# Values of the second attention for all heads at once, token-major and through HBM, with new orders at the opening, between passes and at the end

## The reference, cut to what matters

```python
h = rmsnorm(x, norm_g); proj = h @ w_in            # w_in: 2048 x 10304
aq, ak, av, ag, cq, ckv, kr, bg, mg = split(proj)
# branch A: differential attention, 8 heads, keys/queries 2 x 64, values 128 wide
# branch B: latent attention, 8 heads
q  = (rmsnorm(cq,  q_norm_g)  @ w_uq ).reshape(heads, 128 + 64)    # 512 -> 8 x 192
kv = (rmsnorm(ckv, kv_norm_g) @ w_ukv).reshape(heads, 128 + 128)   # 512 -> 8 x (keys, values)
ob = softmax((q_nope k_nope + rope(q_rope) rope(kr)) * scale) @ values
yb = (ob * silu(bg)) @ w_ob
merged = sigmoid(ga) * ya + sigmoid(gb) * yb
out = rmsnorm(x + merged @ w_out, final_g)
```

## Time and profile before

| | |
|---|---|
| median of 3 runs | 1468.38 us (1468.36 to 1468.58) |
| profiled execution, its own time | 1470.03 us |
| its span, first to last instruction | 1468.2 us |
| mean granted TensorE clock | 0.999 |
| TensorE busy | 98% |
| VectorE, ScalarE, GpSimd busy | 72%, 41%, 3% |
| moved by DMA | 203.75 MB |

### The profile page before, as it was taken

The page is one execution under the profiler, slowest core; times in us unless marked ns, Lnnn a source line. Parts: engine busy times, 40 slices in busy tenths (PEclk is TensorE's granted clock), DMA queues, the critical chain, the costliest instruction groups (busy, mean ns, idle before and its releaser), DMA issues.

```text
span 1468.2 us, 18187 instructions
## 1 busy us (share of the span) xinstructions
PE 1444.1 (98%) x6812; PEld 1201.6 (82%) x6812; DVE 1053.5 (72%) x1423; ACT 606.1 (41%) x786; POOL 45.0 (3%) x58
## 2 busy tenths in 40 slices
PE   7999999999999999999999999999999999999997
PEld 6887888888888888888888888888888888887876
DVE  6867888888877777777776557777777353488956
ACT  5534354444345344453443344443454122324434
POOL 0000000000000011101110000000000000000000
PEclk9999999999999999999999999999999999999999
DMA  8448575767563222322222332222232435517574
GB/s 288 144 150 281 170 259 179 252 194 227 173 189 100 80 79 74 91 79 79 79 72 81 92 87 79 65 72 58 68 121 69 158 116 157 201 44 239 177 245 185
DMA packets 179024, 203.75 MB, mean 139 GB/s; under 512 B 18960, under 2 KB 134800, under 8 KB 178192
## 3 DMA queue, kind: packets, MB, share of 16 engines
q1 hardware_dynamic: 173168, 189.25, 41.8%
q10 hardware_dynamic: 5792, 13.63, 2.4%
HBM read 185.02 MB, written 17.83 MB: 138 GB/s over the span
## 4 chain that ended last, share of the span: by engine, by line
PE 89%; DVE 5%; DMA 3%; SPq 1%; issue 1%; ACT 1%; POOL 0%; DVEq 0%; POOLq 0%; ACTq 0%
PE duo L1959 27%; PE duo L1961 27%; PE duo L1960 27%; PE duo L2012 2%; DMA start_y<-start_columns 1%; PE duo L1986 1%; PE duo L1989 1%; DVE o_lo L1348 1%; DMA spare<-in_w_in_dram 1%; PE duo L2045 1%; SPq L600 1%; PE duo L2039 1%; DMA m_raw<-in_w_in_dram 1%; PE duo L2008 0%; PE duo L2007 0%
## 5 line engine op out<-in xcount | busy, mean ns | idle before, releaser
L1959 PE MATMUL duo<-h_hi,w_hi 128*128 128x512 f32 x656 | 261.0, 398 | 0.3 <-DVE k_hl L1230 0.3
L1961 PE MATMUL duo<-h_hi,w_lo 128*128 128x512 f32 x656 | 256.1, 390 | 0.0
L1960 PE MATMUL duo<-h_lo,w_hi 128*128 128x512 f32 x656 | 255.8, 390 | 0.0
L1225 DVE TENSOR_TENSOR w_lo<-w_raw,w_hi 128x1024 fp32r<-128x1024 f32 (+1 forms) x130 | 156.1, 1202 | 134.6 <-ACT w_hi L707 134.4
L707 ACT ACTIVATE w_hi<-w_raw 128x1024 fp32r<-128x1024 f32 (+1 forms) x130 | 135.5, 1043 | 203.7 <-DMA w_raw<-in_w_ob_dram 65.9
L790 ACT ACTIVATE m_hi<-m_raw 128x2048 fp32r<-128x2048 f32 (+1 forms) x58 | 101.8, 1758 | 143.1 <-PE duo L1961 55.6
L1961 PEld LDWEIGHTS duo<-h_hi,w_lo 128*128 128x128 f32 x656 | 123.1, 188 | 26.9
L1959 PEld LDWEIGHTS duo<-h_hi,w_hi 128*128 128x128 f32 x656 | 123.3, 188 | 24.2 <-DVE k_hl L1230 0.7
L1960 PEld LDWEIGHTS duo<-h_lo,w_hi 128*128 128x128 f32 x656 | 123.5, 188 | 23.5
L1348 DVE TENSOR_TENSOR m_lo<-m_raw,m_hi 128x2048 fp32r<-128x2048 f32 (+2 forms) x59 | 121.0, 2051 | 16.9 <-ACT m_hi L790 16.8
L1959 PE MATMUL duo<-m_hi,h_hi 128*128 128x512 f32 x320 | 126.1, 394 | 4.7 <-ACT post_z L878 2.2
(11 more groups left out here) (293 smaller groups left out, 2846.8 us busy)
## 6 DMA issues: line engine op xcount, KB each, us to landing
m_raw<-in_w_in_dram SPq DMA_DIRECT2D x94, 512.0 KB, 4.6
w_raw<-in_w_in_dram SPq DMA_DIRECT2D x164, 256.0 KB, 3.2
o_raw<-in_w_out_dram SPq DMA_DIRECT2D x34, 512.0 KB, 4.9
w_raw<-in_w_oa_dram SPq DMA_DIRECT2D x32, 256.0 KB, 3.4
sig<-gates SPq DMA_DIRECT2D x8, 1024.0 KB, 6.3
w_raw<-in_w_ob_dram SPq DMA_DIRECT2D x32, 256.0 KB, 3.3
spare<-in_w_in_dram SPq DMA_DIRECT2D x13, 512.0 KB, 4.5
h_raw<-in_w_in_dram SPq DMA_DIRECT2D x13, 512.0 KB, 5.2
```

The costliest lines, as they stand in the source:

```text
L1225: dve.tensor_tensor(w_lo[:, piece.slot, 0:cols], w_raw[:, piece.slot, 0:cols], w_hi[:, piece.slot, 0:cols].bitcast(F32), ALU.subtract).the ...
L1959: pe.matmul(dst, lhs_hi, rhs_hi, start=start, stop=False)
L1960: pe.matmul(dst, lhs_hi, rhs_lo, start=False, stop=False)
L1961: return pe.matmul(dst, lhs_lo, rhs_hi, start=False, stop=stop)
```

## The change

Values of attention B are no longer made per head. Four steps are added to the C steps (20 to 24): with the compressed keys and values as the stationary operand and four heads' value columns of w_ukv (512 wide) as the moving one, they give values token-major for heads 0 to 3 and 4 to 7 in banks of their own. ScalarE copies the banks and stores them in the HBM tensor that held the first attention's values; SP loads each head's strip from there to `vb_raw`, and ScalarE and VectorE split it. The compressed keys and values come ahead of the queries in the C steps. The matmuls of the values in `b_up`, the copy to vT and its transposes go. Beside that orders change: at the opening (x in six parts, weight blocks 0 and 3 split by halves, blocks 1 and 2 loaded ahead of x's tiles 2 and 3), at the ends of the gate groups (`keep_p2` before `merge_hi`), at the starts of passes (`LOW_FIRST`), in the last steps of the output projection, and at the end (the middle store by ScalarE's queue, a shorter variance).

```diff
-A_STEPS, C_STEPS, B_STEPS = 6, 20, 4
+A_STEPS, C_STEPS, B_STEPS = 6, 24, 4
+VB_STEP = 20
+VB_BANKS = ((6, 7, 2, 3), (4, 5, 6, 7))
+B_READS = 3
+        slots = range(M_RAW if shared else OWN_RAW)
+        if st.n == len(steps) - L_STEPS - 1:
+            slots = range(OWN_RAW, M_RAW)
+LOW_FIRST = (V_STEPS, V_STEPS + 1, OUT0 + L_STEPS, OUT0 + L_STEPS + 1, MID_SPLIT)
-TURN_X_AT = {0: (6, 7), 2: (8, 9, 10, 11), 3: (12, 13, 14, 15)}
+TURN_X_AT = {0: (6,), 1: (7,), 2: (8, 9, 10, 11), 3: (12, 13, 14, 15)}
+HALVED = (0, 3)
-X_PARTS = [(0, slice(0, D_MODEL)), (1, slice(0, D_MODEL // 2)), (1, slice(D_MODEL // 2, D_MODEL)),
-           (2, slice(0, D_MODEL)), (3, slice(0, D_MODEL))]
+X_PARTS = [(0, slice(0, D_MODEL // 2)), (0, slice(D_MODEL // 2, D_MODEL)), (1, slice(0, D_MODEL // 2)),
+           (1, slice(D_MODEL // 2, D_MODEL)), (2, slice(0, D_MODEL)), (3, slice(0, D_MODEL))]
...
 SP
+            def b_values_in(h):
...
+                sp.wait_ge(v_lo_ready, h + HEADS)
+                sp.dma_start(vb_raw[:, :, :], v_d[:, bass.ds(h * P, P)].rearrange("(t p) c -> p t c", p=P)
+                             ).then_inc(v_in, 16)
             def b_head(h, odd):
                 for s in range(2):
                     block_piece(Piece(B0 - 2 + s, h, B_STEPS), w_in, 8 * s, h * P + BG)
+                b_values_in(h - 1)
                 up_pieces(h, odd)
             for i, (t, cols) in enumerate(X_PARTS):
-                if i == 3:
+                if i == X_SPLIT + 2:
                     merge_piece(0)
...
-                if i == 4:
                     merge_piece(1)
+                    merge_piece(2)
...
 ScalarE
+            def keep_vb(g):
...
+                for i in range(TOK):
+                    t = (i + 2 * g) % TOK
...
+                    act.activation(vb_keep[:, t, :], bank[VB_BANKS[g][t]][:, :], ACT.Copy).then_inc(v_kept, 1)
+                    act.wait_ge(v_kept, TOK + TOK * g + i + 1)
+                    act.dma_start(v_d[t * P:(t + 1) * P, g * SEQ:(g + 1) * SEQ], vb_keep[:, t, :]).then_inc(v_out[t % 2], 16)
             for s in range(C_STEPS):
+                split_hi(Piece(C0 + s + AHEAD), HALF_PIECE if s == C_STEPS - 1 else 2 * HALF_PIECE)
...
+                if s in (VB_STEP + 1, VB_STEP + 3):
+                    keep_vb((s - VB_STEP) // 2)
             def merge_step(n):
+                if n + 1 in SECOND_END:
+                    keep_p2(MERGE[n].g)
                 if n + AHEAD < N_MERGE:
                     merge_hi(n + AHEAD)
-                if n + 1 in SECOND_END:
-                    keep_p2(MERGE[n].g)
...
 VectorE
             def merge_step(n):
+                if n + 1 < N_MERGE and n in LOW_FIRST:
+                    merge_lo(n + 1)
                 if n + AHEAD < N_MERGE and not ends:
                     merge_sums(n + AHEAD)
-                if n + 1 < N_MERGE:
+                if n + 1 < N_MERGE and n not in LOW_FIRST:
                     merge_lo(n + 1)
...
                 if s == 2 and cur:
-                    dve.wait_ge(used, h * B_STEPS + (B0 + 2))
-                    if prev:
-                        dve.wait_ge(v_turned, h)
-                    dve.tensor_copy(vT[:, :], ACC[0][:, :]).then_inc(acc_read, 1)
...
-                if n >= MID_END - 2:
-                    merge_lo(n + 2)
+                if n == MID_END - 2:
+                    merge_lo(MID_END)
...
             out_u3_c22()
+            merge_lo(MID_END + 1)
             merge_lo(MID_END + 2)
...
 TensorE
+            def token_values(g, half):
+                piece = Piece(C0 + VB_STEP + 2 * g + half)
+                pe.wait_ge(lo_ready, piece.after(0))
+                if not half:
+                    pe.wait_ge(c_lo_ready, LT)
+                for i in range(TOK):
+                    t = (i + 2 * g) % TOK
...
+                    for k in range(2):
+                        hi, lo = tile(piece, k * SEQ, SEQ)
+                        kt = 2 * half + k
+                        last = three(bank[VB_BANKS[g][t]][:, :], c_hi[:, kt, q], c_lo[:, kt, q], hi, lo,
+                                     kt == 0, kt == LT - 1)
...
                 if s == 2 and cur:
                     scores_b(h, 0, prev)
                     scores_b(h, 1, prev)
-                    pe.wait_ge(acc_read, h * 4 + (A_READ0 + 13))
...
-                    turn(vT, TR, v_turned)
...
-                up(piece, 0, ACC[1], 1).then_inc(k_up, 1)
-                pe.wait_ge(acc_read, g + 1)
-                up(piece, P, ACC[0], 1).then_inc(used, 1)
+                up(piece, 0, ACC[1], 0, P).then_inc(used, 1)
                 b_extras(1, h, pair, True, prev)
             def b_gate(h, pair, prev):
                 for s in range(2):
                     if s == 0:
-                        pe.wait_ge(acc_read, h * 4 + (A_READ0 + 12))
+                        pe.wait_ge(acc_read, h * B_READS + (A_READ0 + 12))
```

More of the change, by code:

```diff
@@ L109, in merge_steps @@
         shared = HALF_K + V_SPLIT <= st.n < n_merge - M_RAW or n_merge + L_STEPS <= st.n < len(steps) - L_STEPS
-        st.raw = min(range(M_RAW if shared else OWN_RAW), key=lambda slot: free[slot])
+        slots = range(M_RAW if shared else OWN_RAW)
+        if st.n == len(steps) - L_STEPS - 1:
+            slots = range(OWN_RAW, M_RAW)
+        st.raw = min(slots, key=lambda slot: free[slot])
         turn[st.raw] += 1
@@ L153, with his_by @@
 C_SUMS_AT = (9, 16)
+HALVED = (0, 3)
+def his_by(n):
+    return n + 1 + sum(s <= n for s in HALVED)
 C_NORM_AT = (11, 12, 18, 19)
@@ L158 @@
 PI_DOWN = 3.1415925
-FINAL_STORES = [(1, 1, "last", slice(3 * SEQ, 4 * SEQ)), (0, 1, "middle", slice(MID, 3 * SEQ)), (1, 2, "start", slice(0, MID))]
-X_PARTS = [(0, slice(0, D_MODEL)), (1, slice(0, D_MODEL // 2)), (1, slice(D_MODEL // 2, D_MODEL)),
-           (2, slice(0, D_MODEL)), (3, slice(0, D_MODEL))]
-X_SPLIT = 1
+FINAL_STORES = [(1, "last", slice(3 * SEQ, 4 * SEQ)), (2, "start", slice(0, MID))]
+X_PARTS = [(0, slice(0, D_MODEL // 2)), (0, slice(D_MODEL // 2, D_MODEL)), (1, slice(0, D_MODEL // 2)),
+           (1, slice(D_MODEL // 2, D_MODEL)), (2, slice(0, D_MODEL)), (3, slice(0, D_MODEL))]
+X_SPLIT = 2
 X_HOME = [2, 3, 0, 1]
@@ L369, in hybrid_encoder @@
         g_in_in, gains_in, lambdas_in = sem("g_in_in"), sem("gains_in"), sem("lambdas_in")
-        x_in = [sem(f"x_in{i}") for i in range(TOK + 1)]
+        x_in = [sem(f"x_in{i}") for i in range(len(X_PARTS))]
         pos_in, cst_in = sem("pos_in"), sem("cst_in")
@@ L632, in _ @@
                 block_piece(Piece(C0 + 4 * LT + 2 + s), w_in, 8 * s, BG)
+            for g in range(2):
+                for half in range(2):
+                    value_piece(g, half)
             def b_head(h, odd):
@@ L653, in _ @@
             for t in range(TOK):
-                for ready, n, part_name, cols in FINAL_STORES:
-                    sp.wait_ge((scaled_a, scaled_v)[ready], t * (1, 2)[ready] + n)
-                    part_of = {"last": last_x, "middle": mid, "start": start}[part_name]
+                for n, part_name, cols in FINAL_STORES:
+                    sp.wait_ge(scaled_v, t * 2 + n)
+                    part_of = {"last": last_x, "start": start}[part_name]
                     sp.dma_start(out[0, t * P:(t + 1) * P, cols], part_of[:, t, :]).then_inc(stored, 16)
-            sp.wait_ge(stored, 16 * TOK * len(FINAL_STORES))
+            sp.wait_ge(stored, 16 * TOK * (len(FINAL_STORES) + 1))
         @block.gpsimd
@@ L2301, in _ @@
                     a_head(head, True)
+            def token_values(g, half):
+                piece = Piece(C0 + VB_STEP + 2 * g + half)
+                pe.wait_ge(lo_ready, piece.after(0))
[3 more added lines that the diff above has]
+                    t = (i + 2 * g) % TOK
+                    if not half and g == 0 and i == 0:
+                        pe.wait_ge(o_normed, HEADS)
+                    if not half and g:
+                        if i < 2:
+                            pe.wait_ge(v_kept, TOK + i + 1)
+                        if i == 2:
+                            pe.wait_ge(c_scaled, 2 * LT)
+                    q = slice(t * P, (t + 1) * P)
+                    for k in range(2):
+                        hi, lo = tile(piece, k * SEQ, SEQ)
+                        kt = 2 * half + k
+                        last = three(bank[VB_BANKS[g][t]][:, :], c_hi[:, kt, q], c_lo[:, kt, q], hi, lo,
+                                     kt == 0, kt == LT - 1)
+                    if half and i < TOK - 1:
+                        last.then_inc(v_full, 1)
+                last.then_inc(used, 1)
             for s in range(C_STEPS):
```

215 lines of the change are left out of this document (128 added, 87 removed).

## The result

The kernel after takes 1477.72 us (median of 8 runs, 1473.0 to 1478.9), the kernel before, run beside it, 1469.29 (1468.36 to 1471.13): ratio 1.005, 95% interval 1.0037 to 1.0063. By the medians the change costs 8.4 us; the forecast was 1467.1 and its range ended at 1471.5. Of the eight runs, two stand at 1473.0 with a mean granted clock of 0.998, the other six at 1476.8 and more with 0.993 to 0.995. The profiled execution took 1477.81 us with a span of 1476.0, 7.8 more than before.

A forecast was written before the change was run, and what follows sets the result against it. TensorE, busy 98% of the span, was taken as the bound. Terms -3.9 + 11.6 - 3.2 - 1.6 - 3.7 - 0.5 = -1.3 us took the profiled 1470.03 to 1468.7 and the median to 1467.1; range 1461.5 to 1471.5.

The forecast's parts named there:

- The bound: Whole kernel: TensorE, busy 98% of the span, so what counts is work taken off it and gaps filled or opened.
- Part A: Token-major values: 96 matmuls removed and 96 added, 21.8 us moved; loads, splits, copies and strips covered; nothing gained or lost.
- Part B: Heads of attention B: 32 vT transposes removed, eight turns of 0.49 us each, 3.9 us saved.
- Part C: Heads: value matmuls no longer cover the keys' split before the gate, or head 7's before the output; 11.6 us lost.
- The border of value steps and head 0: Between last value step and head 0: about 4.8 us of ScalarE and VectorE work covered by 5.44 us of matmuls.
- rival 3: Value steps to head 0: ScalarE's table switch drains about 1.38 us beside the load; 1467.9, chance 0.05.
- Part D: Opening: first product about 1.2 us earlier and the 1.96 us idle before 24.98 gone; 3.2 us gained.
- Parts E and F: Gate group ends: copy of post_z ahead of a split, 1.6 us gained; output projection: fewer o_lo, o_x waits, 3.7 gained.
- Part G: Tail: one small VectorE operation less per variance, last store issued 0.4 us sooner; 0.5 us gained.
- The sum: All parts: -3.9 + 11.6 - 3.2 - 1.6 - 3.7 - 0.5 = -1.3 us, median 1467.1.
- Rival 1: Heads: rotary part done earlier, cover not needed; two thirds to all of 11.6 back, 1456 to 1460, chance 0.17.
- Rival 2: Heads: SP late with next head's weights behind the values strip, TensorE waits in seven heads; 1474, chance 0.14.

The follow-up runs named there:

- Kernel 11: Kernel before with token-major values alone, banks changed in every second head and head 7's first quarter of gated values split ahead of the keys: 1466.38 us against 1470.20.
- Experiment 5: Kernel after with unread products in TensorE's wait before the gate (eight in heads 2, 4, 6, fourteen in head 0): 1469.96 us against 1470.09.
- experiment 6: Kernel after with fewer unread products in that wait (two in heads 2, 4, 6, eight in head 0): 1471.47 us against 1470.20.
- experiment 4: Kernel before with the token-major values of the second attention alone, none of the changed orders: 1484.37 us against 1470.20.
- kernels 1 and 5: The first: kernel before with the changed orders alone, values still by head, 1461.72 us against 1470.09; the second: see Experiment 5.
- kernels 9 and 10: Kernel after with two accumulation banks swapped in every second head, 1460.73 us; the same plus head 7's first gated quarter split ahead of the keys, 1458.86; before 1469.17.

## Why the prediction was wrong

**The bound** was read right: TensorE, by what is taken off it and by the gaps.

**Part A (nothing)** held: there is no wait at the value steps and none for a piece or for the strips that come back. **Part B (3.9 saved)** held. The kernel after, head 2, from a score matmul to the next without the transposes:

```profile
975.98 0.39 PE L2093 MATMUL duo<-kr_lo,qr_hl 128*128 128x512 f32 x1
...
981.65 0.39 PE L2088 MATMUL duo<-k_hl,q_hl 128*128 128x512 f32 x1
```

That is 5.67 us for the 25 steps, where rows 4 have 6.16: 0.49 per turn, as forecast. Kernel 11 has 3.8 as a whole.

**Part C (11.6 lost)** is the step that failed, by its second half. Its waits are right in place and nearly in size; with what the next matmul's start shows beyond its pace, after against forecast:

| where | forecast, lost more | in the trace |
|---|---|---|
| head 0 | 2.7 (0.5 was there) | 3.4 in all |
| heads 2, 4, 6 | 2.1 each | 2.1 each |
| heads 1, 3, 5 | 0.3 each | 0.24 each |
| head 7 | 1.7 | 1.7 |
| half pace behind the four long waits | 0 | 1.6 each, 6.5 |

The last line is the mistake. I priced a wait by its length and the 0.1 us by which "the first one after a gap" is slow, and took that for all that a gap does. The old trace could not show me better: it has one stand of that length in the middle of its work, the 2.21 of rows 11, and behind it the matmuls keep their pace, as the window of the kernel before around that restart has it:

```profile
1343.00:1353.00 10.00, 7.79 (x35) 6.21 (x34) 9.90 (x10) 5.67 (x4) 0.00 (x0) 1.00 0.87 303
```

But that stand at full pace, with the 1.96 in the opening, is no ground to leave the lower level out of the range, where the change makes four. Experiment 5 takes the stand away and leaves the gate's start where it was, and the 6.5 go; experiment 6 shortens it to 1.4, and they stay away; experiment 4 shows them with none of the other parts. The bounds that I gave for part C, 0 and 21.8, would have held the 18.1 of waits and half pace, but I put only 1 us of it into the range.

**The border of value steps and head 0** was to be covered, and was: no wait between them. The table's drain (rival 3) didn't show either: ScalarE's exponential starts right behind its load again.

**Part D (3.2)**: x comes in halves of its first two tiles, not in quarters as I wrote. 3.1 measured alone, of which its timeline shows 2.7 behind the third product. The landing was later than I had it (17.96 for 16.3) and the start less early (0.75 for 1.2), but the 1.96 of idle went whole. The kernel after as a whole shows 2.6 at product 3; right in size. **Parts E and F (1.6 and 3.7)**: together 4.1 alone, 1.2 short. The next block's low part costs 0.41 at each of three group ends, so 0.33 to 0.35 is gained of each, 1.0 in all. I took 0.55 since the old idle time of 0.73 was counted with 0.27 around it, and the new one with none. (The old split from 191.54 ends at 193.3, not at the 193.2 that I wrote; the 0.4 to 0.45 fits 193.3.) At the first gate group nothing is gained, as said: its wait is now 1.4 us for m_lo, and TensorE is 2.6 ahead before it and behind it. The output gives 2.9; the waits for o_lo and mg_hi, 1.28 and 0.82 named, are 2.4 with their restarts where I had 1.4. In kernels 1 and 5 the first of the two is missing and 1.0 is left. **Part G (0.5)**: 0.4 in the trace.

**The sum**: with 6.5 for the half pace, 0.6 in E, 0.8 in F and 0.1 in G, -1.3 becomes +6.7 and with 0.6 in D +7.3; the spans differ by 7.8, the medians by 8.4. Kernel 5 tests the sum without the half pace: with all waits still paid it stands 0.1 us under the kernel before, where I had 1.3.

**The rivals.** Rival 1 (the cover isn't needed) is refuted by the 9.0 us of waits; it would have been right had the gate used the other bank (kernels 9 and 10), whose times, 1460.7 and 1458.9, are within 0.7 us of or inside the 1456 to 1460 that I gave it. Rival 2, the only slower one, did not occur: no piece is late. The slower side came from a mechanism that stood in none of the cases, though part C had already named the four stands that bring it on.

## What to carry to other kernels

When cover is taken off a wait, first ask which resource the wait guards. Here it was one accumulation bank of two; turning the two in every second head costs no instruction and gave back some 16 us. When a change makes TensorE stand for two microseconds or more, put a stretch at the lower clock behind each stand into the range, even where the old trace has such a stand without one; filling a stand with products that nobody reads then brings something, though the wait is as long. And time independent parts apart before they are combined: here orders worth 8.4 us hid behind a loss of 14.

## What the runs showed that I had not expected

In the kernel after, the granted clock fell about one microsecond after TensorE had restarted, not during the stand: the first three to five matmuls of the gate run at 0.227, the next eight or so at up to 0.43, and then the pace is back. Heads 2, 4 and 6 of kernel 4 show the same. Its head 0 does not (TensorE; the window is shown with kernel 4):

```profile
912.60 0.80 PE L2011 MATMUL duo<-h_hi,w_hi 128*128 128x512 f32 x1 [3.26 <-DVE k_hl L1286]
913.19 0.63 PE L2012 MATMUL duo<-h_lo,w_hi 128*128 128x512 f32 x1
...
918.24 0.39 PE L2012 MATMUL duo<-h_lo,w_hi 128*128 128x512 f32 x1
```

The gate runs slowly from its first matmul: thirteen steps take 5.64 us in place of 2.95. The window's 0.66 is 6.8 us at the lower level, and as the pace is back near 918.2, the clock fell near 911.4, more than a microsecond before the restart. So after a stand of 3.3 us the loss was 1.6 us in one profile and 2.7 in the other.

Stands of 1.41, 1.43 and 1.49 us in the heads left the pace as it was; those of 1.90, 1.91, 3.26 and 3.27 brought the lower level in both profiles that have them. Yet length alone doesn't decide. The 2.21 of the kernel before had nothing behind it, as shown above, nor had its 1.96 in the opening, while kernel 11, whose opening is the same, has a half-pace stretch behind the same stand, here 2.05 (TensorE; window):

```profile
24.92 0.66 PE L2116 MATMUL duo<-cst,x_tok_in 128*128 128x128 f32 x4 [2.05 <-DVE h_lo L1447]
...
27.17 0.63 PE L2019 MATMUL duo<-m_hi,h_hi 128*128 128x512 f32 x1
```

```profile
15.00:35.00 20.00, 16.65 (x69) 13.06 (x69) 17.18 (x25) 14.51 (x21) 1.08 (x2) 0.91 0.84 285
```

And the two executions of the kernel after at 1473.0 us, with their mean clock of 0.998, are 4.7 under its median; they would fit the same waits with few of the slow stretches, but their timeline was not recorded. What decides between stands of about two microseconds was not tried and stays open.
